# FFN units empty product seven's bank before the last weight sum; loads and splits for head 0, two output weights and the later sums of squares change places

## What is computed

```python
h = h + 0.5 * swiglu_ffn(rmsnorm(h, ffn1_norm), ffn1_w_in, ffn1_w_out)
h = h + stick_breaking_attention(rmsnorm(h, mix_norm), sb_w_qkv, sb_w_o)   # 8 heads of 128
h = h + 0.5 * swiglu_ffn(rmsnorm(h, ffn2_norm), ffn2_w_in, ffn2_w_out)
return rmsnorm(h, final_norm)[frames]

def swiglu_ffn(u, w_in, w_out):            # w_in: 1024 x 5632, w_out: 2816 x 1024
    gate, up = split(u @ w_in)
    return (silu(gate) * up) @ w_out
```

## Time and profile before

| | |
|---|---|
| median of three runs | 1999.19 us (1999.01 to 2000.38) |
| the profiled execution, own time | 1997.4 us |
| its span, first to last instruction | 1995.6 us |
| TensorE busy | 1910.5 us, 96% |
| VectorE busy | 1317.5 us, 66% |
| GpSimd busy | 1075.4 us, 54% |
| ScalarE busy | 754.9 us, 38% |
| mean DMA rate | 137 GB/s |
| mean granted TensorE clock | 0.991 |

### The profile page before, as it was taken

One profiled execution on the slowest core, in us unless ns is written; L12 is line 12 of the kernel. 1 busy time (PEld: TensorE's weight loads), 2 busy tenths in 40 slices (PEclk: granted clock), 3 DMA queues, 4 the chain that ended last, 5 costly groups with the idle time before them and its releaser, 6 DMA issues.

```text
span 1995.6 us, 37428 instructions
## 1 busy us (share of the span) xinstructions
PE 1910.5 (96%) x12508; PEld 1741.4 (87%) x12508; DVE 1317.5 (66%) x1751; ACT 754.9 (38%) x1495; POOL 1075.4 (54%) x1010
## 2 busy tenths in 40 slices
PE   7899999999999999999989999999999999989997
PEld 6899999999999989999989987778777777768875
DVE  5867767776666758333389970296777677666676
ACT  5433343333222335222367761253433343322232
POOL 4456665665555645444477762345656566555560
PEclk9999999999999999999999999999999999999999
DMA  4234434455877411333222212014444444587742
GB/s 128 74 119 146 160 124 154 131 172 194 294 249 243 141 38 59 112 101 111 96 88 84 64 54 64 22 32 138 136 151 154 134 139 150 175 327 242 251 138 95
DMA packets 244611, 273.56 MB, mean 137 GB/s; under 512 B 12976, under 2 KB 176816, under 8 KB 244544
## 3 DMA queue, kind: packets, MB, share of 16 engines
q1 hardware_dynamic: 244544, 272.69, 41.3%
HBM read 179.58 MB, written 93.06 MB: 137 GB/s over the span
## 4 chain that ended last, share of the span: by engine, by line
PE 67%; issue 12%; DVE 7%; POOL 6%; DMA 3%; ACT 3%; SPq 1%; DVEq 0%; POOLq 0%; ACTq 0%
PE psum L1820 22%; PE psum L1822 21%; PE psum L1821 21%; POOL arena L701 5%; DMA arena<-pairs 2%; PE psum L1847 2%; DVE scratch L1450 1%; PE psum L2051 1%; POOL scratch L776 1%; ACT arena L899 1%; DVE arena L1677 1%; DVE arena L1351 1%; DVE scratch L1786 1%; DVE plain L1341 0%; DVE scratch L1401 0%
## 5 line engine op out<-in xcount | busy, mean ns | idle before, releaser
L1820 PE MATMUL psum<-arena 128*128 128x260 f32 (+3 forms) x3908 | 1247.8, 319 | 48.8 <-DVE scratch L1401 11.7
L1822 PE MATMUL psum<-arena 128*128 128x260 f32 (+3 forms) x3908 | 1229.7, 315 | 0.0
L1821 PE MATMUL psum<-arena 128*128 128x260 f32 (+3 forms) x3908 | 1227.1, 314 | 0.0
L1820 PEld LDWEIGHTS psum<-arena 128*128 128x128 f32 x3908 | 740.4, 189 | 110.6 <-issue 34.8
L1821 PEld LDWEIGHTS psum<-arena 128*128 128x128 f32 x3908 | 739.7, 189 | 45.5 <-issue 3.4
L1822 PEld LDWEIGHTS psum<-arena 128*128 128x128 f32 x3908 | 740.0, 189 | 43.8
L701 POOL TENSOR_TENSOR arena<-scratch,arena 128x512 fp32r<-128x512 f32 x365 | 498.0, 1385 | 444.8 <-ACT arena L941 444.8
L1404 DVE TENSOR_TENSOR scratch<-scratch 128x512 f32<-128x512 f32 x200 | 251.7, 1259 | 136.3 <-POOL arena L701 128.9
L941 ACT ACTIVATE arena<-scratch 128x512 fp32r<-128x512 f32 x371 | 215.8, 622 | 263.6 <-DVE scratch L1404 105.4
L1401 DVE TENSOR_TENSOR scratch<-scratch,psum 128x520 f32<-128x520 f32 (+1 forms) x265 | 182.5, 689 | 197.2 <-PE psum L1822 159.0
L793 POOL TENSOR_TENSOR arena<-scratch,arena 128x256 fp32r<-128x256 f32 x280 | 212.7, 779 | 183.1 <-ACT arena L1148 182.9
(11 more groups left out here) (93 smaller groups left out, 1331.0 us busy)
## 6 DMA issues: line engine op xcount, KB each, us to landing
scratch<-w_in_dram SPq DMA_DIRECT2D x88, 512.0 KB, 4.9
pairs<-scratch SPq DMA_DIRECT2D x140, 260.0 KB, 2.8
arena<-pairs SPq DMA_DIRECT2D x35, 1040.0 KB, 8.8
pairs<-scratch SPq DMA_DIRECT2D x140, 256.0 KB, 2.8
arena<-pairs SPq DMA_DIRECT2D x35, 1024.0 KB, 8.9
scratch<-w_out_dram SPq DMA_DIRECT2D x80, 256.0 KB, 3.1
qkv<-scratch SPq DMA_DIRECT2D x48, 260.0 KB, 2.1
scratch<-w_qkv_dram SPq DMA_DIRECT2D x24, 512.0 KB, 4.6
```

Of the source, the lines that this page charges most:

```text
L1820: nc.tensor.matmul(dst, wh, xh, start=start, stop=False, skip_group_check=True)
L1821: nc.tensor.matmul(dst, wh, xl, start=False, stop=False, skip_group_check=True)
L1822: return nc.tensor.matmul(dst, wl, xh, start=False, stop=stop, skip_group_check=True)
```

## The change

1. In all units of both FFNs but the last ones, DVE makes the addition that empties product seven's bank first, and the fourth weight sum (`mix_last`) behind it. Every wait stays with its instruction.
2. SP loads the keys of head 1 before it waits for the stores of the last QKV unit, then the values of head 0, then the queries of head 1; in the loop keys and queries of head hd + 1 come ahead of the values of head hd.
3. ACT splits keys and queries of head 0 inside the last QKV unit, ahead of its first output, rather than behind the unit. The explicit wait ahead of the table load goes.
4. ACT splits the pieces 6 and 7 of `w_o` behind the first and the second square of FFN2's norm, rather than ahead of all squares.
5. In chunk 3 of FFN1's `down`, four groups (rather than two) lie between a group and its sum of squares, and four sums stand at the end.

```diff
@@ SP
             store_qkv(UNITS[QKV] - 1)
+            load_k(1)
             sp_eng.wait_ge(ffns[QKV]["stored"], 64 * BLOCKS[QKV])
             load_v(0)
-            with sp_eng.Fori(1, HEADS) as hd:
-                load_k(hd)
-                load_q(hd)
+            load_q(1)
+            with sp_eng.Fori(1, HEADS - 1) as hd:
+                load_k(hd + 1)
+                load_q(hd + 1)
                 load_v(hd)
+            load_v(HEADS - 1)
@@ ACT, unit(u, last) of QKV
                     product_over(u, 3)
                     weight_hi(n, 6)
+                    if last:
+
+                        for part_of in (("k", 0), ("k", 1), ("q", 0), ("q", 1)):
+                            split(*part_of, 0, 0)
                     first_out(u)
@@ ACT, ahead of the heads
-            act.wait_ge(ffns[QKV]["used"], PRODUCTS * (UNITS[QKV] - 1) + 1)
             nc.scalar.preload_act_table(ACT.Sigmoid)
-            for part_of in (("k", 0), ("k", 1), ("q", 0), ("q", 1)):
-                split(*part_of, 0, 0)
             head(0, 0, first=True)
@@ ACT, behind the heads
-            for dt in range(2, KT):
+            for dt in range(2, 6):
                 split_wo(dt)
...
                 act.wait_ge(o_added, O_ORDER.index((1 - c, kt)) + 1)
+                if c == 0 and kt in (1, 2):
+
+                    split_wo(kt + 5)
@@ DVE, ffn_unit
-                    else:
-                        mix_last(u)
                     product_over(u, 6)
...
                     if last:
                         dve.wait_ge(s["c12"], u + 1)
                         clear(sums_b[0], taken)
+                    else:
+                        mix_last(u)
@@ PE, down_phase
-                        if c >= 2 and dt >= 2:
-                            sums(QKV, c - 2, [dt - 2])
+
+                        lag = 2 if c < 3 else 4
+                        if c >= 2 and dt >= lag:
+                            sums(QKV, c - 2, [dt - lag])
                     if c >= 2:
-                        sums(QKV, c - 2, [KT - 2, KT - 1])
+                        sums(QKV, c - 2, range(KT - lag, KT))
```

More of the change, by code:

```diff
@@ L876, in _, with split @@
         def _(act):
+            def split(name, part, hd, j):
+                dst, src, half, loaded, count, hi = ((k[j], raw_k, TOKENS // 2, k_loaded, 32, k_hi) if name == "k" else
+                                                     (q[j], raw_q, FRAMES // 2, q_loaded, 16, q_hi))
+                cols = slice(part * half, (part + 1) * half)
+                act.wait_ge(loaded, count * (hd + 1))
+                nc.scalar.activation(dst[:, 0, cols], src[:, cols], ACT.Copy).then_inc(hi, 1)
             def take_high(c):
@@ L1177, in _ @@
             units(QKV)
-            def split(name, part, hd, j):
-                dst, src, half, loaded, count, hi = ((k[j], raw_k, TOKENS // 2, k_loaded, 32, k_hi) if name == "k" else
-                                                     (q[j], raw_q, FRAMES // 2, q_loaded, 16, q_hi))
-                cols = slice(part * half, (part + 1) * half)
-                act.wait_ge(loaded, count * (hd + 1))
-                nc.scalar.activation(dst[:, 0, cols], src[:, cols], ACT.Copy).then_inc(hi, 1)
             def split_wo(dt):
```

## The result

The changed kernel takes **1982.53 us** (median of 4 runs, 1981.61 to 1983.35). Of four runs of the kernel before, one fell into the slow state (2110.65), and the other three have the median 1999.19. The ratio is 0.9912, 95% interval 0.9899 to 0.9924, which is 17.6 us; the two medians are 16.7 apart. The forecast was 1974.3, 24.9 less than before: what is missing of that is missing in one place. The profiled executions are 1997.4 and 1982.76, 14.6 apart; their spans 1995.6 and 1981.0.

A forecast was written before the change was run, and what follows sets the result against it. The prediction took TensorE (busy 96%) as the bound, its largest repeated wait being in the second FFN. Gains of 15.7 (FFNs), 2.3 (norm), 3.4 (head 0) and 3.5 (output weights), together 24.9, took 1999.2 to 1974.3 us; range 1968 to 1986.

The forecast's parts named there:

- The forecast's case: Whole kernel: faster by over 0.2%, chance 0.93; 1974.3 us within 1968 to 1986, chance 0.75.
- the signs that were to show it right: Second FFN: no TensorE wait for VectorE's addition, period 38.1 to 38.9; first transposes: no wait above 1.5 us; and others.
- the 39.5 that was to show it wrong: Second FFN: a pair's period above 39.5 us would show the forecast wrong; 38.4 was taken.
- on to the even unit's last sum (21.82, to 1630.05, less the 0.9): Second FFN's weight cycle: the piece from the odd unit's last sum, 21.82 us, shortens by 0.9; whole cycle 38.9.
- The ends of both FFNs: After each FFN's last unit: the 0.9 us of one half counts once more; 1.8 in all, bounds 0 and 2.8.
- Rival (1): Second FFN: the GpSimd lock eats the gain, the wait moves to weight seven, cycle 39.8; 1989.5 us; chance 0.10.
- Rival (2): Norm and head 0: idle stretches bring the lower clock, weights' cycle stays at 38.9; 1982 us; chance 0.10.
- Rival (3): Both FFNs: the addition now ahead delays the last sum by 0.68 us in 40 units; 2017 us; chance 0.03.
- The norm: Start of QKV's norm: with later sums of squares the seventh sum starts sooner; gain 2.3 us, upper bound 2.8.
- The bound of -0.5: Norm before QKV, lower bound of the gain in us: the clock falls in two idle stretches of 1.9 us.
- Head 0: Head 0's start: earlier splits and loads bring the first transposes sooner; gain 3.4 us, bounds 1.3 and 3.7.
- Output weights: Second FFN's norm: later splits of weights 6 and 7 end the first sum's wait; 3.5 us, bounds 3.2 and 3.6.

## Why the prediction was right, and where it failed

The forecast's case held (faster by over 0.2%, within 1968 to 1986), by the other parts and by less than half of the FFN's. Part of that was luck: the first FFN gave 1.5 more than its term, and 1.6 of the norm's gain came with the clock (below). Three of the signs that were to show it right failed: TensorE waits for an addition of VectorE in the second FFN, if another one; the period is 39.47 and not 38.1 to 38.9, just short of the 39.5 that was to show it wrong; and 2.00 us are awaited at the first transposes, where I had allowed 1.5.

**The step that failed** is "on to the even unit's last sum (21.82, to 1630.05, less the 0.9)". That half is 22.02 in the changed kernel (1593.04 to 1615.06). The working inside it was sound: I had VectorE's path to the low part 0.9 shorter, and it is 1.28 shorter, the hidden product taking 1.77 and the two differences 1.29. But I stopped at the differences and took it for granted that what follows comes sooner. What follows is a store, in a queue with 2.1 MB ahead of it, and its landing hangs on the gate load that the last sum releases, 9.17 us before and 9.36 after in this pair. So the cycle is 7.80 + 9.60 + 22.02 = 39.42, and I took 38.4. The row at 1619.35, an addition held by a store, was in the trace before with an idle time of 1.20, and I left it out because VectorE seemed to have time.

**The ends of both FFNs**, forecast at 1.8 by the same 0.9, failed likewise at the second: TensorE's wait there didn't fall. It is 4.87 and 5.05 in two profiles without the swap and 4.87 to 6.09 in six with it (6.09 and 5.59 in the changed kernel's), since the store it hangs on stands behind the down weights. The kernel with the last pair's store ahead shows it. The first FFN's stretch is 651.2 to 652.3 in three profiles without the swap and 648.9 to 651.3 in six with it, on average 1.3 less, where I had 0.9; the two sets overlap, so I claim no more.

**Rival (1)** named the outcome in part: "the wait moves", and the hidden product takes 1.77, as by the lock. But the differences got faster, VectorE's path gained 1.28, the wait moved to a store and not to weight seven, and half a microsecond per pair was left. **Rival (2)** had the measured time, 1982, and not its reason: the clock was not lower (0.992 granted on average, 0.991 before), and the cycle was 39.4 and not 38.9. **Rival (3)** didn't come true, since the addition ended 1.9 us ahead of the sum; the kernel with the product first shows what it would have cost.

**The norm**: 2.5 against 2.3, but not by my sum. Eleven profiles with the later sums have 52.87 to 52.90 for this stretch; with the old ones two have 55.39 and 55.38, and one 53.76. The difference among the three is the clock. Behind the same wait (3.03 to 3.05) the granted clock was 0.59 in the kernel with the FFN part alone, 0.62 before, and 1.00 in the third, the kernel with the old loads and the old distance (busy times of these two, for 4.2 us behind the wait):
```profile
732.70:736.90 4.20, 4.18 (x15) 3.64 (x15) 0.43 (x1) 1.13 (x2) 0.00 (x0) 0.59 0.02 4
```
```profile
729.90:734.10 4.20, 4.19 (x25) 3.83 (x26) 1.13 (x3) 1.76 (x3) 0.00 (x0) 1.00 0.01 4
```
15 matmuls fit into the one, 25 into the other. So the rearranged work gave 0.9, and 1.6 came with the clock, which stayed up behind the shorter wait (1.66 in the changed kernel, at 730.55) in all eleven. That the shorter wait is why it stayed is likely and not shown, since once it stayed behind the longer one too. The bound of -0.5 supposed that two shorter waits bring the lower level as well, which no profile has.

**Head 0**: 3.3 against 3.4 (the stretch varies by 2.8 among eight profiles), and the loads carry most of it. That the loads' old order behind the early splits would be worse than before, I hadn't said. **Output weights**: 3.7 against 3.5; the square runs at 1197.41 and no wait stands at the first sum. The kernel with the FFN part alone has 147.98 for this stretch, 2.2 more than the one before, so the gain varies with the profile that it is taken against.

## What to carry to other kernels

Where a store's landing frees a buffer, follow the loop through the queue: list what is issued ahead of it, in bytes, and price its place by what the queue moves, not by when its data are ready. If its own data come sooner and the loads ahead of it don't, nothing is gained; moving the store ahead of half a megabyte gave 13 us where the swap of two instructions gave 6.6. And a wait for an engine that is itself held by a DMA names the wrong end: look one releaser further before pricing its removal.

## What the runs showed of the hardware

A store behind loads in one queue landed by the bytes ahead of it: at one place it landed at 9.20 and 9.24 us, issued at 5.55 and 4.87, and at another at 7.9 and 8.0, issued at 5.11 and 3.83. The queue moved 350 to 353 GB/s over six us of the burst. The Trainium skill gives about 358 GB/s as one core's share of HBM (DMA: Bandwidth & Descriptors, "Specifications"); these six us agree. Single slices of 1 us inside them show 292 to 395 GB/s, so it isn't a cap on every slice here.

VectorE's second hidden product took 0.72 us on average of 42 where it started alone (before), 1.75 where it followed a sum into GpSimd's subtractions (changed), 1.20 in the kernel that has it first.

The same wait of TensorE, 3.03 to 3.05 us, was followed by its lower clock level in two profiles and by the full one in a third. What decided that, no run here tells.
